# A weight ring whose slots are 64 bytes longer: other start addresses for the same tiles

## The chip, the cores and the metric

The kernel runs on one core of one Trainium2 chip. The metric is the device time of one execution in microseconds; here the median of the runs shown below.

## The reference

Two small transformer stacks run one after the other on one sequence, all in float32. The first puts 16 learned rows ahead of 256 input rows (272 columns of width 1024) and runs two blocks, each a feed-forward (width 2816), a mixer (stick-breaking attention beside a 31-tap convolution, gated) and a second feed-forward, then a final norm and the removal of the 16 rows. The second stack keeps 256 columns and also has two blocks, one with differential attention and one with retention.

```python
def swiglu(x, w_gate, w_up, w_down):
    return (jax.nn.silu(x @ w_gate) * (x @ w_up)) @ w_down
...
    for l in range(DEPTH):
        h = h + 0.5 * swiglu(rmsnorm(h, ffn1_norm[l]), ffn1_w_gate[l], ffn1_w_up[l], ffn1_w_down[l])
        h = h + hybrid_mixer(rmsnorm(h, mix_norm[l]), w_in[l], ...)
        h = h + 0.5 * swiglu(rmsnorm(h, ffn2_norm[l]), ffn2_w_gate[l], ffn2_w_up[l], ffn2_w_down[l])
    h = rmsnorm(h, final_norm)
    return h[:, N_META:]
```

## The kernel before

**Phases.** `PHASES` lists thirteen stages: ffn, mix, ffn, ffn, mix, ffn, final, ffn, da, ffn, ffn, rt, ffn. Activations are kept transposed, with the width on the 128 partitions and the sequence along the free axis: `h` is 8 tiles of 272 columns, and each stage reads its normed input from `u`. Up to the second mixer (`LAST_MIX`) every product has 272 columns; from there on (its last projections included) it has 256.

**Weights.** All weights pass through one ring of four slots (`RING`, line 19). A panel is 128 output columns of a matrix: 8 tiles of 128x128 (`K8`, 1024 columns, 512 KB) or, for the feed-forward's down projection, 11 tiles (`K11`, 1408 columns, 704 KB). There are 680 panels; panel n lies in slot n mod 4 of three tensors, `raw`, `whi` and `wlo` (lines 163 to 165), each with slots of K11 float32 columns. SyncE loads the panel into `raw`. ScalarE copies it with rounding into `whi` (`act_split`, line 399, its instruction on line 405), VectorE writes the rest, raw minus whi, into `wlo` (`dve_split`, line 408, its instruction on line 412). A slot of `raw` is loaded again when the panel four before has been split, and a slot of `whi` is written again when TensorE has used it (`panel_used`).

**Products.** Activations are split in the same way into a high and a low part. Each weight tile is multiplied in three matmuls: high by high, high by low, low by high, in this order, each with its own weight load. `products` (line 383) has them on lines 387 to 389 and sends all three to the same columns of a PSUM bank; `split_products` (line 391, on lines 395 to 397) sends the second to the other half of the bank. A panel of 8 tiles is thus 24 matmuls and one of 11 tiles 33. The feed-forward's loops (`gate_up`, line 619; `out_proj`, line 650) and the mixers' `in_panel` (line 685) and `in_panel2` (line 842) call them; their order is written out by hand, and inside a stage the four slots are used in turn.

**Where tiles lie.** Tensors are allocated one after the other in each partition: `raw`, `whi`, `wlo`, `h`, `u`, small ones, and then an area in which the stages' own tensors share the space (`hid` of the feed-forwards, `qk` and others of the mixers, `dy_hi` and `dw_hi` of the attention, `ry` of the retention). Four slots of 1408 float32 columns are 22528 bytes, `h` is 8704 and `u` 17408 bytes. `tile_of` (line 365) gives the place of a tile of `u` or `hid`: with 272 columns tile k of part p begins at (p * tiles + k) * 1088 bytes and there is no pad; with 256 columns it begins at pad * 4 + (p * tiles + k) * 1024 bytes. The pads are on line 144, and `RY_PAD` is the length of a dummy tensor ahead of `ry`.

```python
U_PAD, HID_PAD, RY_PAD = 112, 24, 144
...
            width, first, at = (T, 0, 0) if y <= LAST_MIX else (SEQ, META, pad)
            at += part * tiles * width
```

Of the kernel before, what the change touches and what calls it, by code (L numbers as in the profile page):

```python
# [17 lines left out]
K11 = HALF * 128  # L18
RING = 4
# [121 lines left out]
DA_PANELS = [(part, n) for part, n in DA_PANELS if 0 <= n < DA_HEADS]  # L141


U_PAD, HID_PAD, RY_PAD = 112, 24, 144


def build(nc, w8, w11, xT, small, cst, lam, outT):
    f32 = mybir.dt.float32
    f32r = mybir.dt.float32r
# [5 lines left out]
    with ctx:  # L155
        def sb(name, shape, dt=f32, where=None):
            return (where or ctx).enter_context(nc.sbuf_tensor(name, shape, dt))
# [3 lines left out]


        raw = sb("raw", [128, RING, K11])
        whi = sb("whi", [128, RING, K11], f32r)
        wlo = sb("wlo", [128, RING, K11], f32r)

        h = sb("h", [128, KD, T])

# [2182 lines left out]
```

## Time and profile before

| | us |
|---|---|
| median of 2 runs | 2204.27 |
| lowest, highest | 2204.13, 2204.4 |
| the profiled execution, its own time | 2210.91 |
| its span, first to last instruction | 2209.1 |

The profile is of one execution. Instruction times are read from the span's start. A matmul overlaps with the next, and its end is modelled, so its duration is longer than the distance from one start to the next; the distance is what adds up to the span. PE is TensorE's matmuls, PEld its weight loads, DVE is VectorE, ACT ScalarE, POOL GpSimd.

In time, the 272-column stages run to about 857 us; the feed-forwards with 256 columns begin near 966, 1153, 1468, 1648 and 2050 us, the differential attention near 1341 and the retention near 1829 us.

### The profile page before, as it was taken

The page shows a single profiled execution, that of the slowest core. Times are in us where ns is not written, and L with a number is a line of the kernel's source. Part 1 is how long each engine was busy: PE and PEld are TensorE (multiplying, and loading weights), DVE is VectorE, ACT ScalarE, POOL GpSimd, SP SyncE. Part 2 cuts the span into 40 slices and gives each one's busy share as a digit, 9 for nine tenths or more (in the row PEclk, how much of TensorE's full clock was granted, in tenths as well). Part 3 has the DMA queues.
Part 4 walks back from the last instruction along what each step waited for, and adds up shares of the span by engine and source line. Part 5 has one row for each costly group of instructions (what it writes and reads, how often), then busy time and mean ns, then how long its engine had stood idle before and what let it go on. Part 6 is the DMA issues. An engine that isn't in the chain of part 4 may idle for free.

```text
span 2209.1 us, 48942 instructions
## 1 busy us (share of the span) xinstructions
PE 2198.0 (99%) x18114; PEld 2180.8 (99%) x18114; DVE 1602.4 (73%) x2450; ACT 1276.6 (58%) x1988; POOL 282.1 (13%) x328
## 2 busy tenths in 40 slices
PE   8999999999999999999999999999999999999999
PEld 8999999999999999999999999999999999999999
DVE  6655997665566579887768767888768766777775
ACT  6444786544444368766546646876556645565662
POOL 0001661100100136220020012010010010101000
PEclk9999999999999999999999999999999999999999
DMA  6555435555455544455555555355556645445553
GB/s 229 174 188 165 159 122 170 167 171 195 155 173 183 179 161 144 144 185 186 190 169 193 195 183 163 124 178 194 195 181 200 219 162 177 161 162 194 188 200 124
DMA packets 100408, 386.68 MB, mean 175 GB/s; under 512 B 11312, under 2 KB 12464, under 8 KB 100304
## 3 DMA queue, kind: packets, MB, share of 16 engines
q1 hardware_dynamic: 99648, 383.89, 52.2%
q8 instruction: 68, 1.11, 0.2%
q0 software_dynamic: 368, 1.26, 0.2%
q14 instruction: 36, 0.29, 0.0%
q10 hardware_dynamic: 288, 0.12, 0.0%
HBM read 384.18 MB, written 1.05 MB: 174 GB/s over the span
## 4 chain that ended last, share of the span: by engine, by line
PE 98%; ACT 1%; DVE 1%; issue 0%; DMA 0%; ACTq 0%
PE bank L387 16%; PE bank L389 15%; PE bank L388 15%; PE bank L395 15%; PE bank L396 14%; PE bank L397 14%; PE bank L759 1%; PE bank L1049 1%; PE bank L1050 1%; PE bank L1051 1%; PE bank L1096 0%; PE bank L709 0%; PE bank L740 0%; PE bank L940 0%; PE bank L943 0%; PE bank L942 0%
## 5 line engine op out<-in xcount | busy, mean ns | idle before, releaser
L412 DVE TENSOR_TENSOR wlo<-raw,whi 128x1024 fp32r<-128x1024 f32 (+1 forms) x677 | 893.3, 1322 | 177.8 <-ACT whi L405 165.4
L405 ACT ACTIVATE whi<-raw 128x1024 fp32r<-128x1024 f32 (+1 forms) x677 | 745.5, 1112 | 164.5 <-PE bank L389 117.2
L387 PE MATMUL bank<-u,whi 128*128 128x272 f32 (+1 forms) x1888 | 549.0, 291 | 7.1 <-DVE u L450 7.1
L389 PE MATMUL bank<-u,wlo 128*128 128x272 f32 (+1 forms) x1888 | 543.7, 288 | 0.0
L388 PE MATMUL bank<-u,whi 128*128 128x272 f32 (+1 forms) x1888 | 541.9, 287 | 0.0
L395 PE MATMUL bank<-u,whi 128*128 128x256 f32 x1888 | 529.2, 280 | 0.2
L397 PE MATMUL bank<-u,wlo 128*128 128x256 f32 x1888 | 527.4, 279 | 0.0
L396 PE MATMUL bank<-u,whi 128*128 128x256 f32 x1888 | 527.4, 279 | 0.0
L387 PEld LDWEIGHTS bank<-u,whi 128*128 128x128 f32 x1888 | 356.9, 189 | 8.0 <-DVE wlo L412 7.3
L388 PEld LDWEIGHTS bank<-u,whi 128*128 128x128 f32 x1888 | 357.0, 189 | 0.9 <-issue 0.2
L397 PEld LDWEIGHTS bank<-u,wlo 128*128 128x128 f32 x1888 | 357.6, 189 | 0.0
L395 PEld LDWEIGHTS bank<-u,whi 128*128 128x128 f32 x1888 | 356.4, 189 | 1.0 <-DVE wlo L412 0.5
L389 PEld LDWEIGHTS bank<-u,wlo 128*128 128x128 f32 x1888 | 356.7, 189 | 0.0
L396 PEld LDWEIGHTS bank<-u,whi 128*128 128x128 f32 x1888 | 354.6, 188 | 0.2
L397 PE MATMUL bank<-hid,wlo 128*128 128x256 f32 x770 | 215.0, 279 | 0.0
L395 PE MATMUL bank<-hid,whi 128*128 128x256 f32 x770 | 215.0, 279 | 0.0
L396 PE MATMUL bank<-hid,whi 128*128 128x256 f32 x770 | 215.0, 279 | 0.0
L437 ACT ACTIVATE u<-h,gain 128x256 fp32r<-128x256 f32 (+1 forms) x88 | 44.1, 512 | 280.6 <-DVE h L1650 136.9
L389 PE MATMUL bank<-hid,wlo 128*128 128x272 f32 (+1 forms) x638 | 183.2, 287 | 0.0
L387 PE MATMUL bank<-hid,whi 128*128 128x272 f32 (+1 forms) x638 | 182.9, 287 | 0.0
L388 PE MATMUL bank<-hid,whi 128*128 128x272 f32 (+1 forms) x638 | 182.3, 286 | 0.0
L397 PEld LDWEIGHTS bank<-hid,wlo 128*128 128x128 f32 x770 | 145.9, 190 | 0.0
(332 smaller groups left out, 3448.8 us busy)
## 6 DMA issues: line engine op xcount, KB each, us to landing
raw<-w SPq DMA_DIRECT2D x552, 512.0 KB, 3.4
raw<-w SPq DMA_DIRECT2D x128, 704.0 KB, 4.1
h<-xT SPq DMA_DIRECT2D x4, 272.0 KB, 4.9
outT<-h SPq DMA_DIRECT2D x8, 128.0 KB, 4.7
consts<-cst POOLq DMA_DIRECT2D x1, 576.0 KB, 4.6
dist<-cst POOLq DMA_DIRECT2D x1, 192.0 KB, 2.7
rdist<-cst POOLq DMA_DIRECT2D x1, 192.0 KB, 3.0
sgain<-small POOLq DMA_DIRECT2D x1, 145.5 KB, 4.8
```

What stands on the lines that cost most here:

```text
L387: pe.matmul(out, w_h, x_hi, start=first, stop=False)
L388: pe.matmul(out, w_h, x_lo, start=False, stop=False)
L389: return pe.matmul(out, w_l, x_hi, start=False, stop=last)
L395: pe.matmul(out[:, 0:SEQ], w_h, x_hi, start=first, stop=False, skip_group_check=True)
L396: pe.matmul(out[:, SEQ:2 * SEQ], w_h, x_lo, start=False, stop=last, skip_group_check=True)
L397: return pe.matmul(out[:, 0:SEQ], w_l, x_hi, start=False, stop=last, skip_group_check=True)
L405: act.activation(whi[:, n % RING, 0:COLS[n]], raw[:, n % RING, 0:COLS[n]], ACT.Copy).then_inc(hi_ready, 1)
L412: dve.tensor_tensor(wlo[:, n % RING, 0:COLS[n]], raw[:, n % RING, 0:COLS[n]], whi[:, n % RING, 0:COLS[n]], ALU.subtract).then_inc(lo_ready, 1)
L437: act.activation(u_at(y, 0, f), h[:, f, win(y)], ACT.Copy, scale=norm_gain(y, f)).then_inc(u_hi_ready, 1)
L759: mm = pe.matmul(bank[5][:, s0:T], vv[:, i, cols], at[:, hd % 2, c0:c0 + w], start=(i == 0 and n == 0), stop=(i == 2 and n == 2), skip_gro ...
L1049: pe.matmul(bank[2 + i][:, :], u_at(y, 0, k, tok.start, tok.stop), w_h, start=(k == 0), stop=False)
L1050: pe.matmul(bank[2 + i][:, :], u_at(y, 1, k, tok.start, tok.stop), w_h, start=False, stop=False)
```

## The change

A slot of `whi` and of `wlo` gets 16 float32 columns more that nothing reads or writes; `raw` keeps its slots. `wlo` then begins 256 bytes later, and all that follows 512 bytes later. The pads are changed by 128, 128 and -128 columns, so that `u` and `hid` in the 256-column stages and `ry` begin at the address they had, modulo 1024 bytes. In the 272-column stages `u` and `hid` have no pad and lie 512 bytes further. No instruction is added, removed or moved.

```diff
-U_PAD, HID_PAD, RY_PAD = 112, 24, 144
+U_PAD, HID_PAD, RY_PAD = 240, 152, 16
+SLOT_PAD = 16
...
         raw = sb("raw", [128, RING, K11])
-        whi = sb("whi", [128, RING, K11], f32r)
-        wlo = sb("wlo", [128, RING, K11], f32r)
+        whi = sb("whi", [128, RING, K11 + SLOT_PAD], f32r)
+        wlo = sb("wlo", [128, RING, K11 + SLOT_PAD], f32r)
```

## Rows read from the trace of the kernel before

**Rows 1.** The page, busy time of each engine, share of the span

```profile
PE 2198.0 (99%) x18114; PEld 2180.8 (99%) x18114; DVE 1602.4 (73%) x2450; ACT 1276.6 (58%) x1988; POOL 282.1 (13%) x328
```

**Rows 2.** The page, granted clock in 40 slices, and the chain that ended last

```profile
PEclk9999999999999999999999999999999999999999
...
PE 98%; ACT 1%; DVE 1%; issue 0%; DMA 0%; ACTq 0%
PE bank L387 16%; PE bank L389 15%; PE bank L388 15%; PE bank L395 15%; PE bank L396 14%; PE bank L397 14%; PE bank L759 1%; PE bank L1049 1%; PE bank L1050 1%; PE bank L1051 1%; PE bank L1096 0%; PE bank L709 0%; PE bank L740 0%; PE bank L940 0%; PE bank L943 0%; PE bank L942 0%
```

**Rows 3.** Waits of TensorE, longest first: us in total, times, longest

```profile
PE bank L387 <- DVE u L450: 7.1, 1, 7.1
PE bank L909 <- DVE dn_lo L1966: 0.4, 1, 0.4
```

**Rows 4.** Windows: width, busy (xcount) of PE, PEld, DVE, ACT, POOL; clock, DMA

```profile
980.00:1080.00 100.00, 100.00 (x851) 100.00 (x851) 79.42 (x124) 61.38 (x107) 0.00 (x0) 1.00 0.57 191
1480.00:1580.00 100.00, 100.00 (x885) 100.00 (x884) 82.98 (x129) 64.97 (x110) 0.00 (x0) 1.00 0.60 201
1660.00:1760.00 100.00, 100.00 (x885) 100.00 (x884) 83.00 (x130) 65.14 (x110) 0.00 (x0) 1.00 0.62 202
1160.00:1260.00 100.00, 100.00 (x851) 100.00 (x850) 82.80 (x137) 64.85 (x114) 0.00 (x0) 1.00 0.57 189
```

**Rows 5.** Timeline of TensorE's matmuls from 1000 us: start, modelled duration, instruction

```profile
1000.20 0.28 PE L395 MATMUL bank<-u,whi 128*128 128x256 f32 x1
...
1001.26 0.28 PE L395 MATMUL bank<-u,whi 128*128 128x256 f32 x1
```

**Rows 6.** The same timeline from 1500 us

```profile
1500.28 0.28 PE L395 MATMUL bank<-u,whi 128*128 128x256 f32 x1
...
1501.30 0.28 PE L395 MATMUL bank<-u,whi 128*128 128x256 f32 x1
```

**Rows 7.** The same timeline, 1442 to 1449 us, last projection of the attention

```profile
1442.09 0.28 PE L876 MATMUL bank<-dy_hi,whi 128*128 128x256 f32 x1
...
1443.34 0.28 PE L876 MATMUL bank<-dy_hi,wlo 128*128 128x256 f32 x1
1443.46 0.59 PE L970 MATMUL bank<-dosq,consts 128*128 128x256 f32 x2
...
1444.12 0.28 PE L876 MATMUL bank<-dy_hi,wlo 128*128 128x256 f32 x1
...
1445.30 0.28 PE L876 MATMUL bank<-dy_hi,whi 128*128 128x256 f32 x1
...
1447.59 0.28 PE L876 MATMUL bank<-dy_hi,whi 128*128 128x256 f32 x1
...
1448.04 0.28 PE L876 MATMUL bank<-dy_lo,whi 128*128 128x256 f32 x1
```

**Rows 8.** Windows: second mixer's last projections, attention, and 1448 to 1826

```profile
930.00:962.00 32.00, 32.00 (x273) 32.00 (x272) 28.44 (x50) 18.59 (x28) 10.27 (x10) 1.00 0.57 187
1341.00:1448.00 107.00, 106.56 (x894) 101.79 (x893) 90.88 (x182) 85.38 (x185) 9.21 (x12) 1.00 0.43 140
1448.00:1826.00 378.00, 377.91 (x3324) 377.05 (x3323) 289.93 (x425) 221.76 (x346) 27.20 (x38) 1.00 0.58 192
```

**Rows 9.** Windows of 272 columns: a gate-and-up loop, a down projection

```profile
400.00:520.00 120.00, 120.00 (x954) 120.00 (x954) 74.49 (x119) 57.99 (x80) 0.00 (x0) 1.00 0.55 181
530.00:580.00 50.00, 50.00 (x401) 50.00 (x400) 23.85 (x24) 18.38 (x18) 7.71 (x11) 1.00 0.47 154
```

**Rows 10.** Timeline of TensorE's matmuls from 431 us, 272 columns

```profile
431.09 0.29 PE L387 MATMUL bank<-u,whi 128*128 128x272 f32 x1
431.22 0.28 PE L388 MATMUL bank<-u,whi 128*128 128x272 f32 x1
431.34 0.29 PE L389 MATMUL bank<-u,wlo 128*128 128x272 f32 x1
```

**Rows 11.** Waits, all engines: the split on VectorE

```profile
DVE wlo L412 <- ACT whi L405: 165.4, 141, 4.4
```

## The prediction

> **What bounds the kernel now.** I read the page first, then the chain, then the waits of TensorE, then the windows, and last the single matmul starts. The page has TensorE busy for 99% of the span, with as many weight loads as matmuls, while VectorE has 73% and ScalarE 58% [rows 1]. The clock is granted in full in every slice, and 98% of the chain that ended last is TensorE, 89% of it on six lines: the three products of `products` and the three of `split_products` [rows 2]. TensorE waited for another engine 7.1 us once, at the start, and no other wait reaches 0.5 us [rows 3]. So the time is the number of matmuls times the distance from one matmul's start to the next, and nothing that feeds TensorE is late. The busy column can't show that distance (matmuls overlap); the count in a window without a wait can.
>
> The counts give the lead of this study. The feed-forwards of the second half all run the same code with 256 moving columns, and their tiles lie at the same addresses. Yet 100 us hold 851 matmuls in two of them and 885 in two others, at the same clock [rows 4]. That is 117.5 ns against 113.0 ns, 4.5 ns or 4%. The starts show it directly: nine steps take 1.06 us in the one (1000.20 to 1001.26) and 1.02 us in the other (1500.28 to 1501.30) [rows 5, 6]. No step stands out, so it is a steady rhythm and no now-and-then stall. And it is sticky: inside the out-projection of the differential attention the steps are 0.11 or 0.12, mean 0.114 from 1442.09 to 1443.34 (11 steps, 1.25 us); then a foreign matmul (L970) comes in between, and from 1444.12 to 1445.30 ten steps take 1.18 us; 3 us later the quick pace is back, four steps in 0.45 us from 1447.59 to 1448.04 [rows 7]. Same tiles, same slots: what flips it is a disturbance of TensorE's rhythm. I call the two paces quick and long. Quick is some of 1344 to 1448 and nearly all of 1448 to 1826 (3324 matmuls in 378 us, 113.7 ns each with its few longer steps) [rows 8].
>
> **What the change does to that.** It adds no instruction, wait, byte of DMA traffic or semaphore. It moves starts of tiles. Within a partition, from the declared sizes, relative to the start of `whi`: before, slot s, tile k of `whi` begins at 5632s + 512k, `wlo` 22528 later, all a multiple of 256. `u` begins at 53760, also a multiple of 256, and in the second half at 448 more with tiles of 1024 bytes, so 192 modulo 256; `hid` and `ry` with their pads lie at 192 too. A weight tile thus always begins 64 bytes after the moving tile, modulo 256, in all slots. After, a slot is 5696 bytes: slot s lies 64s further, `wlo` 256 further, `u` 512 further in the first half and where it was (modulo 1024) in the second. The distance becomes 64, 128, 192, 0 in slots 0 to 3: one panel in four keeps its relation, and the relation changes every 24 or 33 matmuls, where a panel ends. I count modulo 256 because neither quick nor long stretches care that k moves the weights by 512; a modulus of 512 would give whi the same four classes.
>
> Does the distance matter? Two rows say something. In the last projections of the second mixer the 256 columns come from tiles 1088 bytes apart, so every distance in steps of 64 occurs, each for three matmuls: 273 in 32 us, 117.2 ns, the long pace on the mean [rows 8]. In the first half, with 272 columns and tiles again 1088 apart, it is 954 in 120 us, 125.8 ns, and 401 in 50 us, 124.7 ns [rows 9]; the quick pace with 16 columns more at 2.4 GHz would be 113.0 + 6.7 = 119.7. So where the distance keeps changing, no stretch is quick as a whole. Steps differ from matmul to matmul there: 0.13 after 431.09, 0.12 after 431.22 [rows 10], too coarse to name the good distance.
>
> **The sum.** (1) Quick stretch 1448 to 1826: with a disturbed relation each panel I expect the mixed pace, 117.2 to 117.8; 3324 matmuls times (117.8 - 113.7) = +13.6 us. (2) The attention stage 1341 to 1448 holds 894 matmuls; I take two thirds as quick (estimate; the flips of rows 7 show both paces), 600 x 4.3 ns = +2.6 us. (3) Long-paced stretches of the second half, 857 to 1341 and 1826 to 2205, 863 us, some 7300 matmuls at 117.5: at the mixed pace 0. Bounds: all quick, 7300 x -4.5 ns = -33 us; half of the slots at 120.4 (the quick pace plus 7.4 ns, where the first half's 125.8 lies 6.1 ns above its floor of 119.7 on the mean of all distances and the worst of them must lie above that mean), 3650 x 2.9 = +11 us. (4) First half, 850 us at 125.8, some 6750 matmuls: the distances were mixed and stay mixed; only the order at the ends of panels is new. I take 0, with 0.4 ns either way, 2.7 us (the spread between 124.7 and 125.8 is about 1 ns, and only one tile in eight meets a new neighbour). (5) Slot 0 keeps its distance and may fall quick again in stage (1): a quarter of the gain kept at even odds, -2 us. (6) The splits L405 and L412 read and write the moved slots with the same shapes. I price them at 0; the cover is that VectorE is busy 83 of 100 us in the quick window [rows 4] and its split waits for ScalarE 165 us in all [rows 11], a wait that no matmul sees. Without an address effect the gain or loss there is none; with 4% more per split, VectorE would be at 85% and still hidden. Sum: 13.6 + 2.6 - 2 = +14, rounded to +15 for single quick panels elsewhere.
>
> The profiled execution took 2210.91 us around a span of 2209.1; it lies 6.6 us above the median of 2204.27, and its terms shift both alike. Forecast: 2204.3 + 15 = **2219 us**, 0.7% slower. My own range for this case is 2211 to 2226.
>
> **A rule that speaks against it.** The trace shows two paces with one instruction stream [rows 4]. The Trainium skill, page "TensorE: Matmul & The Clock Gate", section "Step-by-step: what each phase is for", says TensorE has two independent read ports, so that loading the next weights takes no read bandwidth from the running matmul. By that rule no address could matter and the time would be 2204; the two paces don't refute it (they could be a rhythm with no memory in it), so it is a rival with a chance of its own. Where a measured pace and the rule differ, the pace decides.
>
> **Rivals.** *A, the other side: the new distances are better.* The long pace may be one in which the weight load keeps meeting the moving tile at distance 64, which a jump of 64 bytes at each panel shakes off. Place: the 863 us at the long pace. For it: flips exist, a disturbance ends the long pace as well as the quick one [rows 7], and slots of other distances were never held for a panel. Against: the mixed rows at 117.2 [rows 8]. All quick: 2204 - 33 = 2171. Two slots of four quick throughout: long-paced stretches gain 16.5, quick ones lose 8, so 2195. It decides from more than 16/49 or a third of the panels quick, below which the kernel is slower.
> *B, two distances are worse than the long pace.* Terms (1) and (2) at (120.4 + 117.8)/2 instead of 117.8 add 3900 x 1.3 = 5, term (3) adds 11: 2219 + 16 = 2235. For it: the first half's 125.8 is further above its floor (6.1 ns) than long is above quick (4.5).
> *C, addresses don't matter,* and the pace is drawn where a stage begins: 2204, within 3 either way; the change then does nothing that it says. A new draw of the paces without regard to addresses could lose the quick stretch (+15) or win another feed-forward of 185 us (-7).
>
> **Chances.** Forecast 0.45, A 0.2, B 0.15, C 0.2. The range, 2186 to 2239, takes in C, A's half gain (2195) with room to 60% of the full one, and B with its first-half term; it leaves out A's full gain. A 2% change, about what a measurement of this kernel can tell from none, is 44 us: faster than 2160 needs more than all quick, slower than 2248 needs 120.4 in every slot (10900 matmuls, +15 +33). Faster 0.02, same 0.93, slower 0.05.
>
> **What would show it.** The count of matmuls in a 100 us window of the third and fourth feed-forward of 256 columns (from 1480 and 1660 us) falls from 885 to 848 to 854 (C: unchanged; A: 865 or more, also in the first ones; B: under 842). The 272-column windows keep 954 within 4. By slots, panels of slot 0 may be quick and others not; if steps are the same in all slots and quick ones remain, the distance is not what matters. VectorE's busy time in these windows stays at 79 to 83 us. I am wrong if the total falls below 2204 by more than the 272-column term.

## The result and the profile after

The changed kernel takes 2228.64 us (2228.2 and 2229.09), against 2204.27: ratio 1.0112, interval 1.0087 to 1.0136. It is slower by 24.4 us. The forecast was 2219, slower by 15, with a range of 2186 to 2239.

The windows of the profile after, TensorE alone (width, busy, matmuls in parentheses, clock, DMA share, GB/s). A count takes in the matmuls under way at both ends, so a pace read from 100 us comes out 0.3% shorter than one read from starts (885 is 113.0 ns by the count and 113.3 by the starts):

```profile
530.00:580.00 50.00, 50.00 (x399) 1.00 0.48 158
980.00:1080.00 100.00, 100.00 (x853) 1.00 0.57 190
1100.00:1150.00 50.00, 50.00 (x424) 1.00 0.47 158
1160.00:1260.00 100.00, 100.00 (x847) 1.00 0.57 190
1480.00:1580.00 100.00, 100.00 (x854) 1.00 0.58 193
1660.00:1760.00 100.00, 100.00 (x854) 1.00 0.58 191
1341.00:1448.00 107.00, 106.67 (x884) 1.00 0.43 140
1472.00:1850.00 378.00, 377.97 (x3206) 1.00 0.57 187
```

The two quick windows of [rows 4] have gone from 885 to 854 matmuls, at the same full clock, and 378 us of nearly the same stretch hold 3206 instead of 3324 [rows 8]. The windows that had the long pace hardly move: 853 for 851, 847 for 851. The cause isn't in what feeds TensorE. Its longest waits are what they were in [rows 3]:

```profile
PE bank L388 <- DVE u L451: 7.3, 2, 7.2
PE bank L910 <- DVE dn_lo L1967: 0.2, 1, 0.2
```

and the split on VectorE waits 166.0 us for ScalarE, as in [rows 11]:

```profile
DVE wlo L413 <- ACT whi L406: 166.0, 141, 4.4
```

The timeline shows what the counts hide. These are the first matmuls of four panels in a row in the first 256-column feed-forward, in slots 2, 3, 0 and 1 (counted from the stage's first panel, which lies in slot 0):

```profile
995.97 0.28 PE L396 MATMUL bank<-u,whi 128*128 128x256 f32 x1
...
998.80 0.28 PE L396 MATMUL bank<-u,whi 128*128 128x256 f32 x1
...
1001.68 0.28 PE L396 MATMUL bank<-u,whi 128*128 128x256 f32 x1
...
1004.41 0.28 PE L396 MATMUL bank<-u,whi 128*128 128x256 f32 x1
```

Twenty-four matmuls take 2.83 us in slot 2 (118 ns each), 2.88 in slot 3 (120 ns) and 2.73 in slot 0 (114 ns). With one instruction stream, the slot now sets the pace. Slot 0 kept the distance 64 between weight tile and moving tile, slot 3 has 0. The window's mean of 117.2 ns conceals a quick panel and a bad one. Over the whole loop the starts give 114.0, 118.9, 117.9 and 120.3 ns in slots 0 to 3. Slot 0 isn't always quick: in the second feed-forward's loop it has 117.9 (the window with 847), and in the down projections 116.8 on the mean.

### The profile page after: what moved, and what is told of

Same layout as the page of the kernel before. It is cut to its first block, busy times and chain, and to the rows that moved or that the text cites. A ratio compares the mean times of both kernels' runs of the same rounds, so it can differ in the third digit from the quotient of the medians.

```text
span 2227.3 us, 48942 instructions
## 1 busy us (share of the span) xinstructions
PE 2216.2 (100%) x18114; PEld 2198.8 (99%) x18114; DVE 1604.0 (72%) x2450; ACT 1277.3 (57%) x1988; POOL 282.1 (13%) x328
## 4 chain that ended last, share of the span: by engine, by line
PE 99%; ACT 1%; DVE 0%; DMA 0%; issue 0%; SPq 0%; ACTq 0%
PE bank L388 16%; PE bank L390 15%; PE bank L389 15%; PE bank L396 15%; PE bank L397 15%; PE bank L398 15%; PE bank L760 1%; PE bank L1050 1%; PE bank L1052 1%; PE bank L1051 1%; PE bank L877 1%; PE bank L1097 0%; PE bank L710 0%; PE bank L741 0%; PE bank L941 0%; PE bank L944 0%
## 5 line engine op out<-in xcount | busy, mean ns | idle before, releaser
L413 DVE TENSOR_TENSOR wlo<-raw,whi 128x1024 fp32r<-128x1024 f32 (+1 forms) x677 | 893.8, 1322 | 178.8 <-ACT whi L406 166.0
L396 PEld LDWEIGHTS bank<-hid,whi 128*128 128x128 f32 x770 | 145.6, 189 | 0.0
```

Of the source, the lines that this page charges most:

```text
L396: pe.matmul(out[:, 0:SEQ], w_h, x_hi, start=first, stop=False, skip_group_check=True)
L413: dve.tensor_tensor(wlo[:, n % RING, 0:COLS[n]], raw[:, n % RING, 0:COLS[n]], whi[:, n % RING, 0:COLS[n]], ALU.subtract).then_inc(lo_ready, 1)
```

## The experiments

All start from the kernel before. Distance means here: where a weight tile begins, less where the moving tile begins, modulo 256 bytes. The attention's `dy` tiles have no pad and stay at 64 in all kernels that change pads alone.

**One distance in all slots.** If the distance itself counts, the slots' paces must appear as whole kernels; if it is the jump at each panel's end, kernels without the jump must be as before. Only line 144 is edited; the other two differ in the numbers (96, 8, 128 and 144, 56, 176).

```diff
-U_PAD, HID_PAD, RY_PAD = 112, 24, 144
+U_PAD, HID_PAD, RY_PAD = 128, 40, 160
```

> The kernel before with U_PAD, HID_PAD, RY_PAD 128, 40, 160: in the 256-column stages every weight tile begins 0 bytes from the moving tile modulo 256, in all slots; no relation changes at a panel's end. Theory (the distance sets the pace; in the changed kernel slot 3, at distance 0, took 120 ns a matmul): every panel of these stages at about 120 ns, 833 matmuls in 100 us, some 9700 matmuls x 3.7 ns more than before, about 2240 us. Rival 1 (the change of relation at each panel costs, not the distance itself): as before, 2204, with quick stretches somewhere. Rival 2 (addresses don't matter): 2204 to 2219.

> Pads 96, 8, 128: distance 128 in all slots of the 256-column stages. Theory (distance): the changed kernel's slot 1 took 118.0 to 118.6 ns, so every panel there at 118.3, 845 in 100 us, about 2222 us, and no quick stretch. Rival 1 (change of relation): 2204 with quick stretches. Rival 2: 2204 to 2219.

> Pads 144, 56, 176: distance 192 in all slots of the 256-column stages. Theory (distance): the changed kernel's slot 2 took 117.6 to 118 ns, so every panel at 117.8, 849 in 100 us, about 2218 us, no quick stretch. Rival 1 (change of relation): 2204 with quick stretches. Rival 2: 2204 to 2219.

Measured: 2246.76, 2234.77 and 2226.53 us, ratios 1.0182 (1.0138 to 1.0225), 1.0127 (1.0085 to 1.0170) and 1.0068 (1.0016 to 1.0119). One window each, in that order:

```profile
1480.00:1580.00 100.00, 100.00 (x836) 1.00 0.54 187
```

```profile
1480.00:1580.00 100.00, 100.00 (x845) 1.00 0.54 189
```

```profile
1480.00:1580.00 100.00, 100.00 (x852) 1.00 0.56 193
```

That is 119.6, 118.3 and 117.4 ns by the count. The order and the paces are as the distance theory had them, and none of the three has a quick window. The kernels are 7, 13 and 9 us above the expected times. Some 6.6 us of each is that I had priced them against the profiled execution, which is that much longer than the median. Their spans are 36.4, 23.7 and 15.7 us above its 2209.1, where 36, 18 and 14 were expected. A jump in distance isn't needed for the loss, and the changed kernel, at 2228.6, is no worse than the mean of the four kernels with one distance each (2228.1).

These three also answer whether it is the distance or one operand's own start that counts. In the changed kernel the weight tiles were moved, here the activations. By the starts, distances 128, 192 and 0 take 118.9, 117.9 and 120.3 ns there and 118.7, 117.8 and 120.0 here. The pace goes with the distance, whichever side moves.

Distance 192 isn't always long. The attention multiplies three weight panels from copies of its own (`dw_hi`, line 1029), 192 from `dy`. They follow on quick matmuls, and 71 steps take 113.3 ns, in the kernel before and in this one with 192:

```profile
1449.00:1456.00 7.00, 7.00 (x64) 1.00 0.49 162
```

```profile
1450.00:1457.00 7.00, 7.00 (x64) 1.00 0.46 156
```

In the changed kernel, at the same distance but after slower matmuls, the same panels take 117.8 ns:

```profile
1452.50:1459.50 7.00, 7.00 (x62) 1.00 0.52 156
```

**Is 256 bytes the period?** Slots of `whi` alone grow by 256 bytes. A first form of this kernel, with the pads as before, was 96 bytes a partition too large for the memory and gave no time; this one gives back 256 bytes of `ry`'s pad.

```diff
-U_PAD, HID_PAD, RY_PAD = 112, 24, 144
+U_PAD, HID_PAD, RY_PAD = 112, 24, 80
...
-        whi = sb("whi", [128, RING, K11], f32r)
+        whi = sb("whi", [128, RING, K11 + 64], f32r)
```

> The kernel before with slots of whi alone 256 bytes longer (64 columns) and RY_PAD 80 to make room, so that ry keeps its place modulo 256; all distances stay 64 modulo 256, but slots of whi differ from each other modulo 1024. Theory (only the distance modulo 256 counts): as before, 2204 to 2219, with quick stretches at 885 in 100 us and slots alike. Rival (a modulus of 512 or 1024 counts): slots differ from each other as in the changed kernel, no quick stretch longer than a panel, 2222 or more.

Measured: 2207.11 us (2203.63 to 2211.29 in 8 runs), ratio 1.0005 (0.9987 to 1.0023). The windows are those of before, quick ones too:

```profile
980.00:1080.00 100.00, 100.00 (x852) 1.00 0.56 191
...
1480.00:1580.00 100.00, 100.00 (x885) 1.00 0.61 202
1660.00:1760.00 100.00, 100.00 (x885) 1.00 0.59 203
```

Longer slots as such cost nothing. For `whi`, which has two of three loads, moves by whole 256 bytes don't count. For `wlo` it was not tried by itself.

**Finer distances.** Pads 104, 16, 136 give 96 in all slots, 108, 20, 140 give 80, and 116, 28, 148 give 48. For `ry` the last two don't: in the built program its dummy tensor's length is rounded up to a multiple of 32 bytes, so `ry` lies at distance 64 in the kernel for 80 and at 32 in the kernel for 48.

```diff
-U_PAD, HID_PAD, RY_PAD = 112, 24, 144
+U_PAD, HID_PAD, RY_PAD = 104, 16, 136
```

> Pads 104, 16, 136: distance 96 in all slots of the 256-column stages, half way between 64 (113.3 or 117.8 ns) and 128 (118.7 ns). Theory A (the memory is met in lines of 64 bytes): as 64 or as 128, or worse because the moving tile straddles one more line: 117.8 to 120, 2218 to 2240 us. Theory B (finer units; between the two lies a distance with a wide margin): quick throughout, 113.3 ns, about 2175 us.

> Pads 108, 20, 140: distance 80. Theory A (lines of 64 bytes): a moving tile that straddles a line more, no better than before, 2204 to 2240. Theory B (quick and long at 64 are the two sides of an edge, so 16 bytes further lies clear of it): quick throughout, 113.3 ns, about 2175 us; then distance 48 is long throughout.

> Pads 116, 28, 148: distance 48. Theory A (lines of 64 bytes): no better than before, 2204 to 2240. Theory B (64 is an edge): quick throughout here and long at 80, or the reverse: 2175 or 2219 us.

Measured: 2233.77, 2237.86 and 2231.51 us, ratios 1.0114 (1.0067 to 1.0162), 1.0133 (1.0086 to 1.0179) and 1.0104 (1.0058 to 1.0150). Distance 80 has one pace in all five feed-forwards. Distance 48 has two, 842 and 859 in 100 us, neither of them quick:

```profile
980.00:1080.00 100.00, 100.00 (x842) 1.00 0.57 186
...
1160.00:1260.00 100.00, 100.00 (x859) 1.00 0.56 192
```

Distance 96 even has three:

```profile
980.00:1080.00 100.00, 100.00 (x836) 1.00 0.54 186
...
1160.00:1260.00 100.00, 100.00 (x850) 1.00 0.57 189
...
1480.00:1580.00 100.00, 100.00 (x845) 1.00 0.56 188
```

All three times are inside what theory A allowed, and theory B (64 lies on an edge, with a quick side) falls: neither neighbour of 64 has the quick pace. Steps of 16 bytes count: 48 and 80 differ from each other and from 64.

The misplaced `ry` is a test that wasn't planned. These are 38 us of the retention's last projection, before (`ry` at 64, long), in the kernel for 80 (at 64) and in the kernel for 48 (at 32):

```profile
1978.00:2016.00 38.00, 38.00 (x325) 1.00 0.53 179
```

```profile
2002.00:2040.00 38.00, 38.00 (x338) 1.00 0.55 183
```

```profile
2000.00:2038.00 38.00, 38.00 (x324) 1.00 0.53 177
```

In a kernel whose feed-forwards all run at 119.3 ns, the retention's projection, which kept 64, is quick, 113.3 ns by the starts.

**Half of the change.** Only the slots of `whi`, then only those of `wlo`, grow by 64 bytes.

```diff
-        whi = sb("whi", [128, RING, K11], f32r)
+        whi = sb("whi", [128, RING, K11 + 16], f32r)
```

> The kernel before with only the slots of whi 64 bytes longer: loads of whi (two of three) at distances 64, 128, 192, 0 by slot, loads of wlo (one of three) at 64. Theory (each load meets the matmul under it on its own): slot 3 near 64's and 0's paces mixed two to one, 119.3 ns, slot 1 118.4, slot 2 117.8; about 2222 us. Rival (only the last, wlo, or the first load counts): 2204 to 2210 with quick stretches, or as the changed kernel, 2228.

> The kernel before with only the slots of wlo 64 bytes longer: one load of three leaves distance 64. Theory (each load on its own): slot 3 118.5 ns, others 117.8 to 118.1, quick stretches broken off at the ends of panels; about 2220 us. Rival (only wlo's load counts): as the changed kernel, 2228; (only whi's): 2204 to 2210.

Measured: 2223.56 us, ratio 1.0082 (1.0060 to 1.0104), and 2216.85 us, ratio 1.0056 (1.0045 to 1.0068). The same two windows, `whi` first:

```profile
980.00:1080.00 100.00, 100.00 (x850) 1.00 0.57 190
1480.00:1580.00 100.00, 100.00 (x850) 1.00 0.57 191
```

```profile
980.00:1080.00 100.00, 100.00 (x857) 1.00 0.58 193
1480.00:1580.00 100.00, 100.00 (x857) 1.00 0.60 196
```

Each half alone ends the long quick stretch, so both kinds of load count; against a median of 2203.8 for the kernel before in these runs, `whi` costs 19.8, `wlo` 13.1 and both 24.4 us. They don't add up, since each alone already ends the quick stretch. Moving `wlo` alone even helps where the pace was long (857 for 851).

The times are near the expected ones (2222 and 2220), but the theory that each load meets its matmul on its own fails by slot. With `wlo` moved, slot 2 should have been long; these are the first matmuls of its panel and of the next, 2.76 us or 115 ns each:

```profile
992.50 0.29 PE L395 MATMUL bank<-u,whi 128*128 128x256 f32 x1
...
995.26 0.28 PE L395 MATMUL bank<-u,whi 128*128 128x256 f32 x1
```

With `whi` moved, slot 3 has 118.1 ns and not 119.3, and slot 2 has 118.3 to 118.8 in the gate-and-up loops but is quick in the down projections, 33 matmuls in 3.74 us or 113.3 ns:

```profile
1098.24 0.28 PE L395 MATMUL bank<-hid,whi 128*128 128x256 f32 x1
...
1101.98 0.28 PE L395 MATMUL bank<-hid,whi 128*128 128x256 f32 x1
```

So where the loads have different distances, the pace isn't a mean of theirs; what rule it follows was not shown.

**A survey of distances, and constant ones with 272 columns.** One kernel gives each stage its own pads. In the 272-column stages, tiles 1088 bytes apart make the distance walk; here the weight tiles of 8-tile panels are 576 bytes apart, inside the same slot, and `hid` tiles 1280 bytes apart, so that it stands still for `u` and `hid`. (The mixers' last projections read other tensors, at other distances.)

```diff
+W_OFF = {0: 0, 1: 48, 2: 16, 3: 32, 4: 16}
+U_PAD = {5: 56, 6: 24, 8: 48, 9: 8, 10: 36, 11: 48, 12: 4}
+HID_PAD = {0: 40, 2: 24, 3: 8, 5: 36, 7: 4, 9: 52, 10: 60, 12: 32}
+HID_COLS = 320
...
+        def weight(w, n, k):
+            step, off = WIDE[n]
+            return w[:, n % RING, off + k * step:off + k * step + 128]
```

> A survey in one kernel: each stage gets its own constant distance. 256-column feed-forwards by pads of u and hid per stage (u distance: 32, 160, 224, 112, 240; hid: 16, 144, 208, 176, 32, in their order). 272-column stages: weight tiles of 8-tile panels 576 instead of 512 bytes apart, so that they keep step with u's tiles (distances 0, 192, 64, 128, 64 in stages ffn, mix, ffn, ffn, mix), and hid tiles 1280 bytes apart (0, 64, 128). Theory (the distance sets the pace, and a constant one leaves the 272-column mean): each of these stages runs at one pace of its own; with 272 columns distance 64 at 119.7 to 124.5 ns instead of 126.1, distance 0 at about 127, 128 at 125.5, 192 at 124.5; with 256 columns all between 113 and 120.5. Rival (272-column stages are bound otherwise, the steps' spread only averages out): 125.3 to 126.1 ns for every distance.

Measured: 2219.47 us in one run. Its total says little; the windows are the result. With 272 columns, u at 0, 64 and 128 (first, second and third line), then hid at 64:

```profile
20.00:140.00 120.00, 120.00 (x951) 1.00 0.57 185
...
400.00:520.00 120.00, 120.00 (x968) 1.00 0.56 183
...
600.00:718.00 118.00, 118.00 (x946) 1.00 0.56 182
```

```profile
530.00:580.00 50.00, 50.00 (x408) 1.00 0.48 158
```

Distance 64 gives 968 for 954 and 408 for 401 [rows 9], 1.5 and 1.7% more; distance 0 gives 951 in 120 us. The ranking isn't the same for both: u at 128 gains (946 in 118 us is the rate of 962 in 120), hid at 128 loses (397 for 401 in 50 us). With 272 columns the distance alone thus doesn't fix the pace; u's tiles and their weights are spaced otherwise than hid's, and whether that is the reason was not tried. With 256 columns, one distance stands out, hid at 144 (second line):

```profile
1160.00:1260.00 100.00, 100.00 (x836) 1.00 0.57 190
1280.00:1330.00 50.00, 50.00 (x443) 1.00 0.51 166
1480.00:1580.00 100.00, 100.00 (x859) 1.00 0.60 196
```

443 in 50 us is 112.9 ns, the quick pace; u at 160, ahead of it, is as bad as distance 0, and u at 224, behind it, is between. By the starts the others have, in ns, 117.2 (16), 118.3 (32, 208), 118.7 (112), 120.0 (176) and 116.7 (240). The rival (a 272-column stage is bound otherwise) falls.

**Two versions built from the survey.** Both hold distance 64 for `u` and `hid` in the 272-column stages. The first leaves 64 in the 256-column stages, the second takes 144.

```diff
+W_OFF = {0: 16, 1: 16, 2: 16, 3: 16, 4: 16}
+RY_PAD = 124
+U_PAD = {5: 28, 6: 28, 7: 28, 8: 28, 9: 28, 10: 28, 11: 28, 12: 28}
+HID_PAD = {0: 24, 2: 24, 3: 24, 5: 4, 6: 4, 7: 4, 8: 4, 9: 4, 10: 4, 11: 4, 12: 4}
```

> A version meant to beat both: the 256-column stages as before (distance 64), and distance 64 held constant in the 272-column stages too (8-tile weight panels 576 bytes apart from 64 bytes into the slot, hid tiles 1280 bytes apart). Theory (distance): the survey measured 124.3 instead of 126.1 ns for u and 123.3 instead of 125.3 for hid at this distance; about 4500 x 1.8 ns and 1584 x 2 ns, 11 us less than before: 2193 us (up to 7 or 15 us more where an execution draws fewer quick stretches, as executions of the kernel before do). Rival (ScalarE's and VectorE's split of the spread-out panels takes longer and TensorE waits): 2200 or more, with waits of TensorE for wlo.

> The same with distance 144 in the 256-column stages (pads 28, 4, 124), where the survey had its down projection quick, 113.4 ns. Theory A (144 is quick always): 113.4 ns for u, hid and ry, some 9700 x 2.9 ns less than before on top of 11 us: about 2165 us. Theory B (144 has two paces like 64, or its quick stretch was a draw): between 2180 and 2215, quick in some stages only, and differing from execution to execution.

Measured: 2199.28 us with distance 64, ratio 0.9986 (0.9969 to 1.0003): the median gains 4.6 us, inside the noise, though its profile has 969 and 408 in the 272-column windows. Its runs say why (us):

```
steady64: 2199.54 2212.37 2198.92 2192.11 2199.32 2198.84 2205.79 2198.48 2199.24 ...
before:   2203.43 2203.84 2203.74 2203.57 2204.46 2204.17 2209.75 2204.08 2203.43 2203.78 2211.38 ...
```

They fall on steps some 7 us apart. A feed-forward of 185 us gains 7 us when it is quick, so a run differs from another by how many stages are quick; that is an inference from totals, since only one execution of each kernel has a trace.

The trace shows what the median hides. The profiled execution (2199.54) has the same quick feed-forwards as that of the kernel before [rows 4], third and fourth:

```profile
400.00:520.00 120.00, 120.00 (x969) 1.00 0.57 185
...
980.00:1080.00 100.00, 100.00 (x852) 1.00 0.57 194
...
1480.00:1580.00 100.00, 100.00 (x885) 1.00 0.60 199
1660.00:1760.00 100.00, 100.00 (x885) 1.00 0.62 200
```

Like for like, its span is 11.4 us shorter (2197.7 for 2209.1), the 11 us expected, and TensorE's waits are those of before. The 272-column edit works as priced. The median shows less because most executions of the kernel before, at 2204, seem to have a third quick feed-forward, and most of this one only two.

With distance 144 it is 2178.36 us (2178.3 to 2178.5), ratio 0.9878 (0.9862 to 0.9895), and the lottery is over. All five feed-forwards are quick:

```profile
975.00:1070.00 95.00, 95.00 (x840) 1.00 0.60 201
...
1150.00:1250.00 100.00, 100.00 (x885) 1.00 0.63 207
1450.00:1550.00 100.00, 100.00 (x884) 1.00 0.61 202
1640.00:1740.00 100.00, 100.00 (x885) 1.00 0.60 203
2030.00:2130.00 100.00, 100.00 (x885) 1.00 0.60 203
```

This version beats the kernel before by 25 us and the changed one by 50. Against the span of the version with 64 it gains 21.2 us, and the three feed-forwards that became quick give 21 of them. That is the count of quick stages again: two at 2199.5, five at 2178.4, 7 us for each. Theory A's 2165 was 13 us too low: it took 2.9 ns off every matmul of the second half, from a median that likely had three feed-forwards quick already. It is just below theory B's 2180, but the four executions agree within 0.2 us, so B's draw is not there either. And `ry` isn't at 144: by the rounding to 32 bytes it lies at 128, and it runs at that distance's pace, 118.6 ns by the starts:

```profile
1954.00:1992.00 38.00, 38.00 (x323) 1.00 0.51 171
```

Whether 144 without the 272-column edits gives the same was not run.

## Why the prediction was right, point by point

**What bounds the kernel: right.** The change added no wait and nothing else, and the whole loss is in the distance between matmul starts.

**Term 1, the quick stretch (+13.6): right.** 3206 for 3324 matmuls is 118 fewer, times the 117.9 ns that they now take: +13.9 us. By the starts, the third and fourth feed-forward are 6.7 and 7.0 us longer. The predicted count of 848 to 854 came out as 854.

**Term 2, the attention (+2.6): two thirds.** 884 for 894 in the same window is 10 matmuls of 120 ns, 1.2 us; from the last matmul of the feed-forward ahead of it to the first of the next it is 120.0 us for 118.2, +1.8.

**Term 3, the long-paced stretches (0): right for the 8-tile panels on the mean, wrong as a picture.** I had them at one mixed pace. In two of the three loops they consist of a quick slot, two near the long pace and a bad one. The down projections lose: 424 for 427 in 50 us, 0.7%. The three feed-forwards are 1.0 us longer, the retention 0.4.

**Term 4, the first half (0, with 2.7 either way): right in size.** The gate-and-up windows keep 954, and the down projection has 399 for 401, about 0.3 us in each 66 us stage. The first 256-column feed-forward begins 1.1 us later.

**Term 5 (-2 for slot 0 falling quick again): right.** In both loops slot 0 is quick, 3.8 ns below the long pace for 528 matmuls, 2 us. It didn't save the total, since slots 1 and 3 (2.88 us a panel) give it back, which the sum had not taken in.

**Term 6 (splits at 0): right,** by the unchanged waits.

**The step that was mis-sized** is the one from the profile to the median: "its terms shift both alike". The spans differ by 18.2 us (2227.3 less 2209.1), which my sum of 15 meets within 3 (1.1 for the first half, 13.7 for the quick pair, 1.8, 1.0 and 0.4 for the rest). The medians differ by 24.4, and 2228.64 is inside the range of 2186 to 2239 but above my own range for this case, 2211 to 2226. The profiled execution of before took 2210.91 us and is itself 6.6 us worse than the median, one of those steps of 7 us. The usual execution of the kernel before most likely had one more quick stage to lose than the one I read: from 2203.8, less the 11.4 of the 272-column stages and less 7 for each of the two feed-forwards left, one gets 2178.4, and the version with five quick ones takes 2178.36. The changed kernel's two runs, one of them the profiled one, lie within 1 us of each other. With that third stage priced the sum would have been 22, and the forecast 2226.

**The rivals.** B (two distances are worse than the long pace) had the right idea: distance 0 costs 119.6 ns by count and 128 costs 118.3, and 120 in slot 3 shows in the changed kernel. Its 120.4 for half of the slots was too much for 128. A (a new distance is better) is wrong for 128, 192 and 0 in the feed-forwards, but right in general: 144 exists. C (addresses don't matter) is refuted by every run but the one that moved slots by a whole 256 bytes. The Trainium skill, page "TensorE: Matmul & The Clock Gate", section "Step-by-step: what each phase is for", has the next weights loaded without taking bandwidth from the running matmul; here 836 or 885 matmuls fit in 100 us depending on where the weight tile begins, so the measurement differs from the page.

What stays open is the mechanism below the distance. The runs show that with 256 columns the relation of the two reads, modulo 256 bytes, sets the pace or the few paces that are possible, that both kinds of weight load count, and that some distances have several steady paces. Why 144 settles into the quick one in every feed-forward, and what picks between paces at 48, 64, 96 and 192, was not shown.

## What to carry to other kernels

Where TensorE never waits, compare the number of matmuls in windows of the same code: a difference of some per cent at the same clock is a pace, and it can hang on where weight tiles and moving tiles begin relative to each other. Give the ring and the activations strides that keep one distance for all tiles, then sweep that distance in steps of 16 bytes, as it costs only pads. Read the addresses in the built program while you do: here a pad tensor was rounded up to 32 bytes, and three kernels had one tensor at another distance than meant. If runs of a kernel fall on steps a few us apart, look for a stage with two paces before pricing a change against one profile.

## What the hardware showed that I had not expected

- With 256 columns, 100 us hold 836 (distance 0), 841 (80), 845 (128), 852 (192), 851 or 885 (64), and 885 (144) matmuls of the same shape at a granted clock of 1.00.
- A distance can have more than one steady pace: 48 has 842 and 859, 96 has 836, 845 and 850 in 100 us, all in one execution. 192, long in every feed-forward, kept the quick pace of the matmuls ahead of it for three panels of the attention (64 matmuls in 7 us).
- With `whi` and `wlo` at different distances from the moving tile (64 and 192), a slot took 115 ns, less than either the long pace of 64 or that of 192.
- With 272 columns, a constant distance of 64 gives 968 or 969 instead of 954 matmuls in 120 us.
